# The second half's mixer block: the first half's rows turned by VectorE in 32x32 blocks instead of by TensorE

## The reference

```python
def pool_mixer(x, w_in, w_group, scale, w_out):
    u = (x @ w_in).reshape(b, t, 4, 256)
    # group g: trailing mean over 2, 4, 8 or 16 tokens, minus u itself
    y = jnp.einsum('btgc,gce->btge', pooled - u, w_group).reshape(b, t, D_MODEL)
    return (y * scale) @ w_out

h = layer_norm(ALPHA * h + pool_mixer(h, ...), ln_mix_g, ln_mix_b)
gate, up = jnp.split(h @ w_gu, 2, axis=-1)
h = layer_norm(ALPHA * h + (jax.nn.silu(gate) * up) @ w_down, ln_ffn_g, ln_ffn_b)
```

## Time and profile before

| | us |
|---|---|
| median of 3 runs (1639.79 to 1641.46) | 1639.8 |
| profiled execution | 1641.42 |
| its span, first to last instruction | 1639.6 |
| TensorE busy | 1629.3 (99%) |
| VectorE busy | 1043.1 (64%) |
| GpSimd busy | 640.4 (39%) |
| ScalarE busy | 606.8 (37%) |

### The profile page before, as it was taken

One profiled execution on the slowest core, in us unless ns is written; L12 is line 12 of the kernel. 1 busy time (PEld: TensorE's weight loads), 2 busy tenths in 40 slices (PEclk: granted clock), 3 DMA queues, 4 the chain that ended last, 5 costly groups with the idle time before them and its releaser, 6 DMA issues.

```text
span 1639.6 us, 18911 instructions
## 1 busy us (share of the span) xinstructions
PE 1629.3 (99%) x7233; PEld 1349.7 (82%) x7233; DVE 1043.1 (64%) x1095; ACT 606.8 (37%) x837; POOL 640.4 (39%) x440
## 2 busy tenths in 40 slices
PE   9999999999999999999999999999999999999998
PEld 7888878888888888888888888888888888888886
DVE  7758756888445565554756777667544443467866
ACT  6225443545434434433533333333333332322330
POOL 0420025016358677664456765666720000341000
PEclk9999999999999999999999999999999999999999
DMA  9563456434367666556756666666577544564542
GB/s 365 201 253 132 154 201 235 163 146 179 116 200 235 204 209 226 195 195 210 254 194 206 211 197 199 210 214 187 177 242 257 189 147 140 199 218 167 205 142 95
DMA packets 192010, 322.45 MB, mean 197 GB/s; under 512 B 7856, under 2 KB 135984, under 8 KB 183216
## 3 DMA queue, kind: packets, MB, share of 16 engines
q1 hardware_dynamic: 152224, 289.25, 51.7%
q10 hardware_dynamic: 37520, 23.60, 4.6%
q0 software_dynamic: 2176, 8.39, 1.3%
HBM read 218.97 MB, written 102.24 MB: 196 GB/s over the span
## 4 chain that ended last, share of the span: by engine, by line
PE 98%; DVE 1%; ACT 0%; DMA 0%; issue 0%; DVEq 0%; SPq 0%; ACTq 0%
PE acc L1262 44%; PE acc L1292 19%; PE acc L1101 10%; PE turn L1262 7%; PE acc L1135 7%; PE turn L1292 6%; PE turn L1135 3%; PE acc L1167 1%; PE acc L1180 0%; PE turn L1090 0%; DMA raw<-w_out 0%; DVE sums L1743 0%; ACT st_mix L1340 0%; DVE mov L1703 0%; PE acc L1191 0%; DVE z L2146 0%
## 5 line engine op out<-in xcount | busy, mean ns | idle before, releaser
L1262 PE MATMUL acc<-fa,wf 128*128 128x512 f32 x1584 | 362.8, 389 | 0.0
L1262 PE MATMUL acc<-fb,wf 128*128 128x512 f32 x1584 | 362.8, 389 | 0.0
L1262 PEld LDWEIGHTS acc<-fa,wf 128*128 128x128 f32 x1584 | 297.3, 188 | 61.7
L1262 PEld LDWEIGHTS acc<-fb,wf 128*128 128x128 f32 x1584 | 297.4, 188 | 61.6
L1292 PE MATMUL acc<-dw,da 128*128 128x512 f32 x1386 | 315.3, 389 | 0.0
L1292 PEld LDWEIGHTS acc<-dw,da 128*128 128x128 f32 x1386 | 260.2, 188 | 53.9
L1883 DVE TENSOR_TENSOR wf<-wt,wf 128x512 fp32r<-128x512 f32 x132 | 134.2, 1020 | 139.7 <-ACT wf L1477 139.7
L1883 DVE TENSOR_TENSOR wf<-wr,wf 128x512 fp32r<-128x512 f32 x176 | 187.4, 1071 | 38.9 <-ACT wf L1477 38.5
L927 POOL TENSOR_TENSOR wt<-wr,wt 128x512 f32<-128x512 f32 x88 | 140.8, 1600 | 150.8 <-DVE wf L1883 150.6
L1477 ACT CAST wf<-wr 128x512 fp32r<-128x512 f32 x176 | 108.6, 618 | 214.6 <-PE acc L1262 211.8
L1101 PE MATMUL acc<-mov,split 128*128 128x512 f32 x768 | 179.5, 393 | 0.0
(11 more groups left out here) (152 smaller groups left out, 1809.1 us busy)
## 6 DMA issues: line engine op xcount, KB each, us to landing
wr<-w_gu SPq DMA_DIRECT2D x44, 1024.0 KB, 5.2
dar<-af_dram SPq DMA_DIRECT2D x56, 704.0 KB, 4.5
af_dram<-g ACTq DMA_DIRECT2D x32, 512.0 KB, 5.7
fs<-hf_dram SPq DMA_DIRECT2D x14, 1024.0 KB, 5.6
dt_raw<-w_down SPq DMA_DIRECT2D x22, 512.0 KB, 5.8
wt_dram<-dt_t SPq DMA_DIRECT2D x22, 512.0 KB, 3.7
sa<-af_dram SPq DMA_DIRECT2D x22, 512.0 KB, 8.3
af_dram<-sx SPq DMA_DIRECT2D x22, 512.0 KB, 4.5
```

Source lines behind the costliest of these rows:

```text
L1262: mm = nc.tensor.matmul(dst, wf[:, slot, a, k, :], fa[half][i][:, v, :, k, :], start=i < 2 and k == 0 and n3 == 0, stop=k == KC - 1 and n3 ...
```

## The change

The 64 turns on TensorE are gone. In steps 1 and 2 of `mixer_block(1)`, behind the pooling, VectorE turns pairs 0 and 1 (`turn_pair`); in steps 4 and 5, ahead of the pooling, pairs 2 and 3. The rows come from `h_dram`, in blocks of 32 columns, back into their own place in `zm`. Block 0's tiles are loaded by SyncE, block 1's by ScalarE (`load_second_tile`), two tiles each at the end of steps 1 and 2. ScalarE scales pair p-2 in step p and does all four norms of block 1 in step 0. SyncE's list is reordered.

```diff
-        def turned_block(n):
+        def pair_place(pi, a):
+            return zm[a][:, pi].rearrange("p (g n) -> p g n", g=QT) if pi < TT else nat_gu[:, a]
+        def turned_block(pi, n):
             a, kh = ((1, 0), (0, 0), (0, 1), (1, 1))[n]
-            src = nat_gu[:, a].rearrange(...)
-            return st_gu[:, n].rearrange("p k (g t) -> p g k t", t=Q), src
+            src = pair_place(pi, a).rearrange(...)
+            return st_of(pi)[:, n].rearrange("p k (g t) -> p g k t", t=Q), src
# SyncE, load_pair
+                elif pi > TT:
+                    sp.wait_ge(turn_done, TT * pi)
                 else:
-                    sp.wait_ge(turn_done, TT * pi)
+                    sp.wait_ge(rows_stored[a][pi], 16)
# SyncE, order
             for j in range(TT):
                 store_h(0, j)
+            load_in(1, 2)
+            load_pair(0, 0)
+            load_pair(1, 0)
             load_x(3, 2)
             load_x(3, 3)
             for j in range(TT):
                 store_h(1, j)
-            load_in(1, 2)
+            load_pair(2, 0)
+            load_pair(3, 0)
+            load_in(1, 3)
             load_z(2, 0)
             load_z(3, 0)
-            load_in(1, 3)
             load_z(2, 1)
             load_z(3, 1)
+            load_mix(1, 0)
             load_z(2, 2)
             load_z(3, 2)
-            load_mix(1, 0)
+            load_mix(1, 1)
             load_z(2, 3)
             load_z(3, 3)
-            load_mix(1, 1)
             load_mix(1, 2)
# TensorE: turn_part and the hook between are gone, with the waits on turn_taken
# ScalarE
+            def load_second_tile(pi):
+                act.wait_ge(rows_stored[1][pi], 16)
+                src = h_dram.rearrange(...)[0, pi, 1]
+                for n in range(QT):
+                    nc.scalar.dma_start(pair_place(pi, 1)[:, n], src[n]).then_inc(z_landed[1][pi], 16)
                     if h and 2 <= p <= TT + 1:
-                        take_turn(p - 2, 2)
-                        take_turn(p - 2, 3)
-                    if h and 1 <= p <= TT:
-                        take_turn(p - 1, 0)
-                        take_turn(p - 1, 1)
+                        scale_turned(p - 2, 0)
+                        scale_turned(p - 2, 1)
...
-                    if h and p < 2:
-                        norm(1, 2 * p)
-                        norm(1, 2 * p + 1)
+                    if h and p in (1, 2):
+                        load_second_tile(2 * p - 2)
+                        load_second_tile(2 * p - 1)
+                    if h and p == 0:
+                        for j in range(TT):
+                            norm(1, j)
# VectorE
+            def turn_pair(pi):
+                if pi < 2:
+                    dve.wait_ge(d_lo_ready, NP)
+                else:
+                    dve.wait_ge(st_stored[pi % 2], 16 * (pi // 2))
+                    dve.wait_ge(ss_made, 4 * (pi - 1))
+                for step, n in enumerate(TURN_ORDER):
+                    if step % 2 == 0:
+                        dve.wait_ge(z_landed[1 - step // 2][pi], 16 + 16 * QT)
+                    dst, src = turned_block(pi, n)
+                    nc.vector.transpose(dst, src).then_inc(turn_done, 1)
+                    if h and p in (4, 5):
+                        turn_pair(p - 2)
                     if p >= 1:
                         pool(2 * h + STEPS[p - 1][0], STEPS[p - 1][1])
+                    if h and p in (1, 2):
+                        turn_pair(p - 1)
```

More of the change, by code:

```diff
@@ L411, in st_of @@
             return st_mix[pi % 2] if pi < 4 else st_gu
-        def pair_rows(pi, a, kk):
-            return zm[a][:, pi].rearrange("p (r c) -> p c r", c=KT)[:, kk]
+        def pair_place(pi, a):
+            return zm[a][:, pi].rearrange("p (g n) -> p g n", g=QT) if pi < TT else nat_gu[:, a]
         TURN_ORDER = (0, 3, 1, 2)
-        def turned_block(n):
+        def turned_block(pi, n):
             a, kh = ((1, 0), (0, 0), (0, 1), (1, 1))[n]
-            src = nat_gu[:, a].rearrange("p g (r c) -> p g c r", c=KT)[:, :, kh * KC:(kh + 1) * KC]
-            return st_gu[:, n].rearrange("p k (g t) -> p g k t", t=Q), src
+            src = pair_place(pi, a).rearrange("p g (r c) -> p g c r", c=KT)[:, :, kh * KC:(kh + 1) * KC]
+            return st_of(pi)[:, n].rearrange("p k (g t) -> p g k t", t=Q), src
         HF_OF = (0, 3, 4, 1, 5, 6, 2)
@@ L610, in load_pair @@
                             sp.wait_ge(rows_stored[e][row], 2 * 16)
+                elif pi > TT:
+                    sp.wait_ge(turn_done, TT * pi)
                 else:
-                    sp.wait_ge(turn_done, TT * pi)
+                    sp.wait_ge(rows_stored[a][pi], 16)
                 src = h_dram.rearrange("(h a j g t) (q c) -> h j a g q t c", h=2, a=2, j=TT, g=QT, q=QT)[half, j, a]
                 for n in range(QT):
-                    sp.dma_start(nat_gu[:, a, n], src[n]).then_inc(pair_landed[a], 16)
+                    sp.dma_start(pair_place(pi, a)[:, n], src[n]
+                                 ).then_inc(z_landed[a][pi] if pi < TT else pair_landed[a], 16)
             def load_form(q):
@@ L1080, in chunk_is_split, with hidden @@
                 pe.wait_ge(w_lo_ready, after_fold(c))
[L1082 to L1093, removed]
+            def hidden(c, x_of, slot, banks, before=None):
                 chunk_is_split(c)
@@ L1105, in hidden @@
                         mm.then_inc(chunk_done, 1)
-                    if between is not None:
-                        between(m)
             def outward(h, t):
@@ L1118, in outward @@
                         pe.wait_ge(added, added_by(h - 1, 4, m))
-                        pe.wait_ge(turn_taken, 2 * TT * TT)
                     elif t == 1:
@@ L1213, in mixer_block @@
                         pe.wait_ge(added, added_by(h - 1, 6, 2 * i + 1))
[L1215 to L1220, removed]
+                    hidden(c_in(h, i), mov_of(b), c_in(h, i) % 2, p % 2, x_is_split if first and p == 0 else None)
                     if first:
@@ L1248, in product @@
                     if n == 0:
-                        pe.wait_ge(turn_taken, 2 * TT * TT)
+                        pe.wait_ge(added, added_by(LAST_HALF, 4, 2))
                     else:
@@ L1324, in x_hi @@
                                ).then_inc(x_hi_ready, 1)
[L1326 to L1345, removed]
             def store_turned(pi):
@@ L1350, in store_turned @@
                                     ).then_inc(st_stored[pi % 2], 16)
+            def load_second_tile(pi):
+                act.wait_ge(rows_stored[1][pi], 16)
+                src = h_dram.rearrange("(h a j g t) (q c) -> h j a g q t c", h=2, a=2, j=TT, g=QT, q=QT)[0, pi, 1]
+                for n in range(QT):
+                    nc.scalar.dma_start(pair_place(pi, 1)[:, n], src[n]).then_inc(z_landed[1][pi], 16)
             def scale_turned(pi, kh):
                 act.wait_ge(turn_done, TT * pi + 3 + kh)
+                if pi == 0:
+                    act.wait_ge(mix_gb_kept, 1)
                 for k in range(KC):
-                    both, kk = st_gu[:, 2 * kh:2 * kh + 2, k, :], kh * KC + k
+                    both, kk = st_of(pi)[:, 2 * kh:2 * kh + 2, k, :], kh * KC + k
                     nc.scalar.activation(both, both, ACT.Identity, bias=mix_b_sb[:, kk:kk + 1],
@@ L1790, in add_rows @@
                     if t in (1, 3):
-                        dve.wait_ge(z_landed[t // 3][m], 16 * (h + 1))
+                        dve.wait_ge(z_landed[t // 3][m], 16 * (1 + (QT + 1) * h))
                     out_is_done(dve, h, t, m)
@@ L1997, in turn_block @@
                     dve.wait_ge(pair_landed[0], 16 * QT * (pi - TT + 1))
-                dst, src = turned_block(TURN_ORDER[step + place])
+                dst, src = turned_block(pi, TURN_ORDER[step + place])
                 nc.vector.transpose(dst, src).then_inc(turn_done, 1)
```

## The result

The changed kernel takes 1663.4 us (median of 4 runs, 1662.1 to 1665.3), the one before 1640.6 beside it (4 runs): ratio 1.014, 95% interval 1.0125 to 1.0156. It is 23 us slower, where 8 us less was forecast; the range ended at 1637.0. The profiled execution's span is 1660.3 us against 1639.6. A ratio's 95% interval stands in square brackets.

What follows compares the result with a forecast made beforehand. TensorE, busy 99% of the span, was taken as the bound. Gain 11.3 less 3.2 lost (2 lateness, 1.2 clock) is 8.1; 1641.42 less 8.1 is 1633.3, less 1.6 to the median is 1631.7 us; range 1628.0 to 1637.0.

Steps and rivals of the forecast that it cites:

- the 11.3 us that the change removes: TensorE, second half's mixer block: 7.4 us of turns, 2.4 of waiting for ScalarE, 1.6 of clock drop; the gain's ceiling.
- The sum from 1641.42 to 1631.7: Profiled execution 1641.42 us less 8.1 gain is 1633.3, less 1.6 because that execution lies above the median: 1631.7.
- I take 0.6 because both medians agree: ScalarE's 16 new DMA issues priced at 0.6 us each: 2.4 a tile, 9.6 in all, ends 6 and 28.
- About 360 at full share, and 4 MB are 12 us of it. They fit: DMA in the 98 us stretch: 203 GB/s at share 0.56, so the 4 MB of added reads fit in 12 us.
- The added issues on SyncE: SyncE's 16 issues, some 10 us, ahead of its loads: priced at nothing; 7 to 10 us if cover fails.
- Step 1: ScalarE's norms 4.63 us, stage and split to 219.5; first reload issued by 222, tile landing at 229 us.
- the rival of the late tile: ScalarE's reloaded tile lands late, hurting TensorE from 235 us; 1643 us if 26 us after last issue; chance 0.06.
- Step 3: ScalarE issues two tiles (4.8 us) before splitting p=4's weights: ready 245.7, wanted 245.4, so 0.3 us late.
- The rival of 0.14: ScalarE's issues cost 1 us or more; p=4 weights 3 to 6 us late, clock drop; 1635.5 us; chance 0.14.
- The transposes of step 2: VectorE's 16 block transposes at 1.17 us each, 18.7 us; four take 4.7 us, first pair turned by 242.9.
- the rival of 0.03: GpSimd stretches VectorE's transposes by 6.80/3.79, 15 us more on VectorE; 1643.5 us, slower; chance 0.03.
- Steps 4 to 6: GpSimd's sums and stores delay VectorE's pooling: p=7 at 278.4 against 278.1, t=1 at 303 against 299.9 us.

Runs made afterwards that it cites:

- The last experiment: Sums of pair 3 alone put in bytes of their own, in two pieces, against the version with a third buffer; 1630.4 us, ratio 0.9941.
- the version with a third buffer: Changed kernel with 32-row reloads all begun by SyncE, plus pair 2's turned rows in bytes of their own; 1634.3 us, ratio 0.9964.
- the third version with unused copies: Kernel before plus 16 unused copies of x begun by ScalarE, slowest dimension 4, each tile in its own bytes, no wait between batches; 1656.0 us, ratio 1.010.
- the 54 executions above: Kernel before, unchanged, run beside the experiments: 41 executions took 1639.5 to 1640.7 us at clock 0.999, 13 took 1641.1 to 1642.1 at 0.998.

## Why the prediction was wrong

- **What bounds the kernel, and the 11.3 us that the change removes: right for the profiled execution.** The last experiment takes 11.5 us from it, and 9.3 from the median.
- **The sum from 1641.42 to 1631.7 counts 1.6 us twice.** It books the clock drop as removed, and then subtracts 1.6 again because the profiled execution lies that much above the median. The typical execution has no such drop. Without the double count the same working gives 1633.3 us, still in the range, so this did not turn the outcome.
- **"I take 0.6 because both medians agree", 9.6 us in all with ends at 6 and 28: this is the step that failed.** It was 36.1, outside both ends. Without it the kernel takes 1637.3 us (issues back at 0.6 us, which also lets the tiles land early) or 1640.2 (slow shape, SyncE as issuer), so it is 23 to 26 of the 31.7 us by which the forecast was off, and the reversal from gain to loss. A median over issues that are spread out says nothing of 16 in two batches. In the earlier trace rows SyncE's reloads, which have the same slowest dimension of 4, reach 1.294 us. A steady 128 KB at the 96 GB/s seen here takes 1.37; I read that end of the row as an outlier, and it was near the price of one queue at its limit. With two queues on the same four engines it is 2.6. The forecast's own sign of being wrong, issues over 1 us, came true: their median is 2.16.
- **"About 360 at full share, and 4 MB are 12 us of it. They fit": failed for the same reason.** That divides by 16 engines. At 96 GB/s 4 MB are 44 us.
- **The added issues on SyncE, "I put nothing": held for the queue behind it.** Its last eight took 15.4 us instead of 5, and nothing on TensorE waited for what stood behind. But the w_in chunk behind it landed at 250.5 us, 18.3 after its issue, where the forecast wanted it at 245: the long wait hid that. And while they ran they halved the rate of ScalarE's first batch.
- **Step 1 (norms, reload issued by 222, tile lands at 229):** norms 4.64 us; ScalarE's first issue began at 219.96 (219.5 was worked out), its fourth at 222.41, and the tile landed at 236.0. By its own working, the rival of the late tile begins to hurt at 235 us. Whether it did is hidden: ScalarE's blocked stage was late first. Where late landing stands alone, with SyncE as issuer, it costs 5.6 us.
- **Step 3 (split of the p=4 weights 0.3 us late, "more if an issue costs more"): right place, wrong size.** It was the place of the 22 us. The rival of 0.14 named this chain and priced it at 3 to 6 us, since it went to 1 us an issue and stopped.
- **The transposes of step 2: right.** Sixteen took 17.0 us (groups of four 4.01 to 4.35) against 18.7 forecast. In the version with a third buffer four of them ran beside GpSimd's additions (235.2 to 239.6 us) and took 4.41, where that rival wanted some 8.4, so the rival of 0.03 is out.
- **Steps 4 to 6 (GpSimd's chain, p=7 0.3 us late, t=1 3 us late): the mechanism was right, the place and size at p=7 not.** With the reloads repaired it shows: 4.7 and 3.0 us at p=7, where the stores of pairs 0 and 1 took 8.3 to 13.4 us to land, against 10.9 at most in the earlier trace rows; with p=7 freed, 2.5 us at t=1. That is the forecast's "TensorE ends up 2 to 3 us late at the worst place". The forecast 1631.7 us was not quite reached with the reloads alone repaired (1634.6), and was passed only by the last version (1630.4).

## What to carry to other kernels

Before a DMA issue is put on an engine that also computes, work out how long its transfer takes alone on the DMA engines that its shape can use, from a window's share and GB/s; if several follow each other, that time and not the median of the issue is the price, and the engine's whole order stands behind it. To this add what else runs on those engines at the time. Cut such copies so that the slowest dimension lets more engines work (32 in place of 4 brought the share from 0.27 to 0.99 here), or give them to an engine with nothing urgent behind them. When buffers are shared, list for each late write which store it waits for: here two stores had to be taken off one after the other, and the first hid the second.

## What the runs showed that I had not expected

- A DMA issue can block its engine: the first few of a batch take some 0.5 us, the later ones 1.2 to 1.3 with one queue (1.27 in the version where SyncE begins all) and 2.6 with two queues in reloads of this shape; 5.15 is the longest of the change, 6.3 in the unused copies. Such long ones stand where large transfers run beside them. In the third version with unused copies the second batch took 20.2 us with no reload by SyncE: 3 MB of loads and a 0.75 MB store had gone out at 224.9 to 233.4, and the DMA share from 226 to 238 us is 0.89 to 1.03. How the four engines divided their time is not shown.
- While nothing else runs, reloads whose slowest dimension is 4 move at 96 GB/s and those of 2 at 48, both in rows of 1 KB.
- A short wait of TensorE brings a lower clock in some cases and not in others. A granted clock between 0.50 and 1.00 is time at both levels, 1.2 and 2.4 GHz. After 1.73 us of waiting: 0.76, x24 in 7.07 us. After 2.53 (third buffer): 0.77, x24 in 7.33. After 2.96 (32 rows, all by SyncE): 0.87 over x48, 12.8 us, where an unbroken x48 takes 11.07. But after 1.73 at the same place with 32-row unused copies: 1.00, x24 in 5.74; after 1.75 in the changed kernel: 1.00, x48 in 11.18; after 1.87 with SyncE as issuer: 1.00, x24 in 5.73. One kernel does both, as the 54 executions above tell. After 22.2 us, with the clock at 0.50 from 253 us on, x192 took 46.43 against 43.68 unbroken (SyncE as issuer): 2.8 us, little more than after 2.96.
